# Products of zeros on TensorE ahead of four blocks of a GLA/NSA decoder step

## The chip, the cores and the metric

The kernel runs on one core of a Trainium2 chip. The metric is the device time of one execution in microseconds; of several runs the median counts. All matrix products run on TensorE (PE in the rows), whose granted clock the profile records: 1.00 is 2.4 GHz and 0.50 is 1.2 GHz.

## The reference

One inference step of a two-layer decoder trunk with 512 prompt tokens and 8 decode tokens, width 1024. The first layer mixes with gated linear attention (GLA), the second with native sparse attention (NSA); behind each stands a squared-ReLU MLP of width 4096.

```python
for i in range(DEPTH):                      # DEPTH = 2
    hp = rms_norm(xp, norm_mix[i]); hs = rms_norm(xs, norm_mix[i])
    ...                                     # i = 0: gla_mixer, i = 1: nsa_prompt / nsa_sample
    x = x + mixer(rms_norm(x)); x = x + mlp(rms_norm(x))

def gla_mixer(h, s0, w_in, w_gate2, b_gate, g_out, w_out):
    z = h @ w_in                            # q, k, v, r and the 16 gate-rank columns gr
    log_alpha = log_sigmoid(gr @ w_gate2 + b_gate) / GLA_TAU
    o, s = gla_scan(...)
    o = rms_norm(o, g_out)
    return (o * silu(r)) @ w_out, s

def sq_relu_mlp(h, w_up, w_down):
    u = relu(h @ w_up)
    return (u * u) @ w_down
```

The NSA layer projects h to queries, six kinds of keys and values and the gates, attends in three branches, and ends in `o @ w_out`.

## The kernel before

The 520 tokens lie as columns: the residual `xT` is [128, 8, 520], eight chunks c of 128 channels. Each weight matrix and each activation is split into a high part (fp32r) and a rest, and a block of 128 output columns is the sum of high x high, high x rest and rest x high (`split_products`). A block goes through eight steps k (one chunk of channels each); a step is three products in two halves of 260 tokens, so six matmuls.

TensorE writes into four PSUM slots of two banks. A table made ahead of time gives each product its slot and its turn. `claim` makes TensorE wait until the slot's earlier product has been read, `await_product` is the reader's side. Each engine has its own instruction stream, written out in order; semaphores tie them together.

A norm goes like this: ScalarE squares the chunks, VectorE adds the squares, TensorE multiplies the sum by a matrix of 1/1024 (`mean_square`, line 2038), ScalarE takes the root (line 992), VectorE the reciprocal (line 1469) and then the eight normed chunks (line 1485). ScalarE rounds each chunk to its high part (lines 1023 and 1251). The rest parts of chunks 0 to 3 are made by GpSimd (lines 799 and 876), those of chunks 4 to 7 by VectorE once all eight normed chunks are done (lines 1515 and 1711). TensorE's next block takes them step by step: a wait per k on `mixed_rest_ready[k // 4]`.

Four blocks matter here, in order of time:
- `grank`, the gate-rank block of the GLA layer, behind the first norm: 16 output columns, slot 3; the products `gq` follow. Its weights' rest part comes from GpSimd (line 794).
- `gout` 0, the first block of the GLA output projection, slot 0. Ahead of it stand the last decode products and `omd`, the mean square of the decode rows (line 2185). Its operand needs the last head's norm on VectorE (lines 1469, 1616 to 1636). In the order of TensorE's stream it first waits for its weights (`ow_rest_ready`), then claims, then waits for the operand at k = 0 and again at k = 6.
- `z` 0, the first block of the NSA projection, behind the third norm, slot 0. The weights are ready beforehand.
- `nout` 0, the first block of the NSA output projection, slot 2. Ahead of it stand the turned decode rows `d_ot` (line 2515), their copy on VectorE (line 2008), the high part (line 1451) and the rest (line 2015, `no_rest_ready`).

`identb` is a 128x128 bf16 identity (VectorE, line 1500) and `zerosb` 512 bf16 columns of zeros (GpSimd, line 773); both are made at the start of the kernel. The kernel before already uses such a product in three places to clear a bank.

Of the kernel before, what the change touches and what calls it, by code (L numbers as in the profile page):

```python
# [28 lines left out]
DC = D // 128  # L29
# [68 lines left out]
def trunk(nc, ins, outs):  # L98
    ctx = ExitStack()
    with ctx:  # L100
# [34 lines left out]
        identb = carve("identb", 64).bitcast(BF16)  # L135
        zerosb = carve("zerosb", 256).bitcast(BF16)
# [53 lines left out]
        gh_part = [part("gh_high", at["go"][0], DC, T), part("gh_rest", at["hT"][0], DC, T)]  # L190
# [3 lines left out]
        wgr_part = [part("wgr_high", at["cum"][0], DC, RANK), part("wgr_rest", at["wgr"][0], DC, RANK)]  # L194
# [113 lines left out]
        slot = [ctx.enter_context(nc.psum_tensor(f"slot{s}", [128, 2, 512], F32)) for s in range(4)]  # L308
# [8 lines left out]
        free = [sem(f"free{s}") for s in range(4)] + [sem("free_out_bank"), sem("free_cmp_bank")]  # L317
# [16 lines left out]
        mixed_rest_ready = [sem("mixed_first_rest_ready"), sem("mixed_second_rest_ready")]  # L334
# [273 lines left out]
        def where(name, i=None, n=0):  # L608

            if i is None:  # L610
                return turn[name]
            slots, base, per = turn[name]
            s = n % len(slots)
            return slots[s], i * per + (base[s] + n // len(slots))

        def claim(eng, name, i=None, n=0):

            s, k = where(name, i, n)
            if not isinstance(k, int) or k > 0:
                eng.wait_ge(free[s], k)  # L620
            return slot[s], full[s]
# [1406 lines left out]
        def _(pe):  # L2028
            mm = nc.tensor.matmul
# [12 lines left out]
            def mean_square(n):  # L2042
                pe.wait_ge(sum_ready, DC * (n + 1))
                ps, fu = claim(pe, ("ms", n))
                dense(ps, lambda k: C("mean_d"), lambda k: sq_sum, 1).then_inc(fu, 1)

            pe.wait_ge(ident_in, 32)
            for c in range(DC):
                if c % (DC // 2) == 0:
                    pe.wait_ge(x_in[c // (DC // 2)], 16)  # L2050
                ps, fu = claim(pe, ("xt", c))
# [3 lines left out]
                    .then_inc(fu, 1)  # L2055
            pe.wait_ge(consts_in, 32)
            mean_square(0)
            def split_products(ps, weights, x, wait=None):

                (high, rest), (x_high, x_rest) = weights, x  # L2060
                for k in range(DC):
                    if wait is not None:
                        wait(k)
                    for w, m in ((high, x_high), (high, x_rest), (rest, x_high)):
                        for a in range(2):
                            last = mm(ps[0:w.shape[2], a, 0:HT], w[:, k, :], m[:, k, HT * a:HT * a + HT],  # L2066
                                      start=k == 0 and w is high and m is x_high, stop=k == DC - 1 and w is rest)
                return last

            pe.wait_ge(wgr_rest_ready, 1)  # L2070
            ps, fu = claim(pe, "grank")
            split_products(ps, wgr_part, gh_part, wait=lambda k: pe.wait_ge(mixed_rest_ready[k // 4], k % 4 + 1)).then_inc(fu, 1)

            def gla_products(name, first_block, count):

# [11 lines left out]
            for h in range(GH):  # L2087
                ps, fu = claim(pe, ("gate", h))
# [3 lines left out]
            for n in range(20):  # L2092
# [4 lines left out]
                ps, fu = claim(pe, ("gv", n))  # L2097
                for k in range(DC):
                    high, rest = gw_high2[:, q % 2, k, :], gw_rest2[:, q // 2, k, 256 * (q % 2):256 * (q % 2) + 256]
                    for hp, w in ((0, high), (0, rest), (1, high)):  # L2100
                        last = mm(ps[0:rows, 0, 0:256], gh_part[hp][:, k, 128 * t:128 * t + rows], w,  # L2101
                                  start=k == 0 and w is high and hp == 0, stop=k == DC - 1 and hp == 1)
# [20 lines left out]
            for what, h in GLA_STEPS:  # L2123
                if what == "kt":

                    pe.wait_ge(gdec_ready, h + 1)
                    ps, fu = claim(pe, ("kt", h))
# [3 lines left out]
                elif what == "at":  # L2131

                    pe.wait_ge(kp_ready, h + 1)
                    ps, fu = claim(pe, ("at", h))
                    mm(ps[:, 0, :], identb, zerosb, start=True, stop=False, skip_group_check=True)
                    for c in range(TT):
                        for s in range(NSUB):
# [4 lines left out]
                                      skip_group_check=True)  # L2142
                    last.then_inc(fu, 1)
                elif what == "u":

                    pe.wait_ge(kt_ready, h + 1)
                    ps, fu = claim(pe, ("u", h))
# [4 lines left out]
                elif what == "o":  # L2152
# [3 lines left out]
                    ps, fu = claim(pe, ("o", h))  # L2156
                    for v in range(2):
                        for c in range(TT):
                            o = ps[:, v, 128 * c:128 * c + 128]
                            last = mm(o, gv[:, c, DV * h + 128 * v:DV * h + 128 * v + 128], at2[:, h % 2, c, :],  # L2160
                                      start=True, stop=c == 0)
# [4 lines left out]
                elif what == "vb":  # L2166
# [3 lines left out]
                    ps, fu = claim(pe, ("vb", h))  # L2170
# [3 lines left out]
                elif what == "om":  # L2174
                    pe.wait_ge(osq_ready, h + 1)
                    ps, fu = claim(pe, ("om", h))
# [5 lines left out]
            ps, fu = claim(pe, "omd")  # L2182
# [4 lines left out]
            for n in range(DC):  # L2187
                t, columns = TILE_GLA_OUT + n // 4, slice(128 * (n % 4), 128 * (n % 4) + 128)

                def wait(k):  # L2190
                    if n == 0 and k == 0:
                        pe.wait_ge(go_rest_ready["heads"], 3)
                        pe.wait_ge(go_rest_ready["decode"], 1)
                    elif n == 0 and k == 2 * GH - 2:
                        pe.wait_ge(go_rest_ready["last_head"], 1)

                pe.wait_ge(ow_rest_ready, n + 1)
                ps, fu = claim(pe, ("gout", n))
                split_products(ps, (go_high_w[n % 4], gw_rest2[:, t % 2, :, columns]), go_part, wait).then_inc(fu, 1)
                if n % 4 == 3:  # L2200
                    pe.wait_ge(fu, where(("gout", n))[1] + 1)
                    pe.sem_inc(tile_used[t % 2], 1)
# [23 lines left out]
            for what, n in steps():  # L2226
                kind, j = chunks[n]
                if what == "z":
                    pe.wait_ge(pw_rest_ready, n + 1)
                    ps, fu = claim(pe, ("z", n))  # L2230
                    split_products(ps, pw_part[n % 2], u_part,
                                   wait=(lambda k: pe.wait_ge(mixed_rest_ready[k // 4], DC // 2 + k % 4 + 1)) if n == 0 else None).then_inc(fu, 1)
                elif what == "nm":
                    pe.wait_ge(z_ready, n + 1)
                    ps, fu = claim(pe, ("nm", n))
                    dense(ps, lambda k: C("mean_h"), lambda k: sq4[:, n % 4, :], 1).then_inc(fu, 1)
                elif what == "sw":
                    pe.wait_ge(normed, turned[n] + 1)
                    ps, fu = claim(pe, ("sw", n))
                    dense(ps, lambda k: C("swap"), lambda k: z4[:, n % 4, :], 1).then_inc(fu, 1)  # L2240
                elif what == "gt":
                    pe.wait_ge(pw_rest_ready, len(chunks) + 1)
                    ps, fu = claim(pe, ("gt", 0))
                    split_products(ps, [w[:, :, 0:48] for w in pw_part[0]], u_part).then_inc(fu, 1)
                elif what == "gates":
                    pe.wait_ge(z_ready, len(chunks) + 1)
                    ps, fu = claim(pe, ("gates", 0))
                    for t in range(5):
                        rows = 128 if t < TT else NS
                        last = nc.tensor.transpose(ps[0:rows, 0, 48 * t:48 * t + 48], z4[0:48, 0, 128 * t:128 * t + rows],  # L2250
                                                   ident[0:48, 0:48])
                    last.then_inc(fu, 1)
                else:
                    if is_roped[n]:
                        pe.wait_ge(roped, turned[n] + 1)
                    pe.wait_ge(z_ready, n + 1)
                    src = nk[:, {4: 0, 5: 1, 8: 2, 9: 3}[j], :] if j in (4, 5, 8, 9) else z4[:, n % 4, :]
                    ps, fu = claim(pe, ("tok", n))
                    for t in range(TT):
                        nc.tensor.transpose(ps[:, 0, 128 * t:128 * t + 128], src[:, 128 * t:128 * t + 128], ident)  # L2260
                    nc.tensor.transpose(ps[0:NS, 1, 0:128], src[:, NP:T], ident).then_inc(fu, 1)

            for what, r, sp in compression_steps():
# [4 lines left out]
                if what == "pb":  # L2268

                    pe.wait_ge(pe_sum_ready, r + 1)  # L2270
                    ps, fu = claim(pe, ("pb", r))
                    for c in range(2):
                        last = mm(ps[:, 0, c:c + 1], pe_sum[:, 128 * c:128 * c + 128], C("tri")[:, 127:128],
                                  start=True, stop=True)
                    last.then_inc(fu, 1)
                elif what == "x":
                    pe.wait_ge(st_copied, 8 * r + sp + 1)
                    ps, fu = claim(pe, ("xt2", r, sp))
# [4 lines left out]
                elif what == "m":  # L2283
# [5 lines left out]
                    for half in range(2):  # L2289
                        for wp, xp in ((0, 0), (0, 1), (1, 0)) if g == 4 else ():  # L2290
                            last = mm(psh[:, 0, 0:256], xt_part[xp][:, sp % 2, half:half + 128],
                                      w1_part[wp][:, 8 * half + sp, :], start=sp == 0 and half == 0 and wp == xp,
                                      stop=sp == 7 and half == 1 and wp == 1)
                        for c in range(2) if g < 4 else ():
                            for wp, xp in ((0, 0), (0, 1), (1, 0)):
# [3 lines left out]
                                          stop=sp == 7 and half == 1 and wp == 1)  # L2299
# [4 lines left out]
                elif what == "ht":  # L2304
                    s, k = where(("hid", r))
# [4 lines left out]
                elif what == "c":  # L2310
# [3 lines left out]
                    ps, fu = claim(pe, ("c", r))  # L2314
# [13 lines left out]
                elif what == "cn":  # L2328
                    pe.wait_ge(kcz_ready, r + 1)
                    ps, fu = claim(pe, ("cn", r))  # L2330
# [8 lines left out]
            for what, n in attention_steps():  # L2339
                if what == "cs":  # L2340
                    p, t = n // 4, n % 4
                    ps, fu = claim(pe, ("cs", n))
                    sc = ps[:, 0, 0:2 * GQ * CW]
                    mm(sc, identb, hidden_b[:, t:t + 1, :].to_broadcast([128, 2 * GQ, CW]), start=True, stop=False,
                       skip_group_check=True)
                    for g in range(GQ):
                        last = mm(sc.rearrange("p (e g n) -> p e g n", e=2, g=GQ)[:, :, g, :],
                                  nq[:, 4 * p + g, 128 * t:128 * t + 128], kcz[:, p, :], start=False, stop=g == GQ - 1,
                                  skip_group_check=True)
                    last.then_inc(fu, 1)  # L2350
                elif what == "ct":
                    pe.wait_ge(pc_ready, n + 1)
                    ps, fu = claim(pe, ("ct", n))
# [4 lines left out]
                elif what == "s":  # L2358
# [6 lines left out]
                    ps, fu = claim(pe, ("s", n))  # L2365
                    scores = both_kinds(ps, t)
                    kinds = [slice(0, 2)] if t < 2 else [slice(0, 1), slice(1, 2)]
                    for part in (ks_high, ks_rest):
                        for a in kinds:
                            mm(scores[:, a, :], qs[:, n // 8 % 2, e, g, :], part[e][:, p, a, 0:w], start=part is ks_high,  # L2370
                               stop=False, skip_group_check=True)
                    for a in kinds:
                        last = mm(scores[:, a, 128 * t:128 * t + 128], identb,
                                  future_b.unsqueeze(1).to_broadcast([128, a.stop - a.start, 128]), start=False, stop=True,
                                  skip_group_check=True)
                    last.then_inc(fu, 1)
                elif what == "t":
                    pe.wait_ge(p_ready, n + 1)
                    ps, fu = claim(pe, ("t", n))
# [7 lines left out]
                elif what == "pv":  # L2387
                    p, t, g, _ = unit(2 * n)
# [125 lines left out]
            for m in range(8):  # L2514
                last = mm(ps[:, 0, 32 * m:32 * m + 32], o_rows[:, 128 * m:128 * m + 128], fold, start=True, stop=True)
            last.then_inc(fu, 1)
            pe.wait_ge(no_rest_ready, DC + 1)
            for n in range(DC):
                t, columns = TILE_NSA_OUT + n // 4, slice(128 * (n % 4), 128 * (n % 4) + 128)
# [114 lines left out]
```

## Time and profile before

| | us |
|---|---|
| median of three runs | 1972.5 |
| lowest, highest | 1971.04, 1978.53 |
| the profiled execution | 1968.85 |
| its span | 1967.1 |
| TensorE busy | 1790.7 |
| VectorE, ScalarE, GpSimd busy | 895.2, 678.4, 446.3 |
| mean granted clock of TensorE | 0.946 |

All times inside the profile count from the start of the span. A busy TensorE is not one at its peak: a matmul's recorded length contains its way through the array and overlaps with the next one, so the distance from start to start tells the pace.

### The profile page before, as it was taken

To read this page: it belongs to the slowest core of one execution; us is meant where nothing else is said; L and a number is where in the kernel's file an instruction comes from. 1 tells how busy PE (TensorE), PEld (TensorE's weight loads), DVE (VectorE), ACT (ScalarE), POOL (GpSimd) and SP (SyncE) were. 2 spreads that over 40 slices of the span, in tenths; PEclk is the share of its full clock that TensorE was granted. 3 is DMA by queue.
4 is the path that set the end of the run, shared out by engine and by line. 5 is a ranking of instruction groups with operands and counts; after the bars stand their busy time and mean duration, and the time that the engine had idled before them with its cause. 6 is when DMAs were issued, how large, how long until landed. Compare 5 with 4: busy or idle time off the path is not lost.

```text
span 1967.1 us, 32578 instructions
## 1 busy us (share of the span) xinstructions
PE 1790.7 (91%) x13592; PEld 1626.9 (83%) x13592; DVE 895.2 (46%) x1347; ACT 678.4 (34%) x1131; POOL 446.3 (23%) x381
## 2 busy tenths in 40 slices
PE   4999997999999997999799998898877999999996
PEld 2989876999999997989677786676644999999996
DVE  6051254744444345446622523877422644434343
ACT  3353233332313232323233422777641332313230
POOL 3244224100000002334212221787702100000000
PEclk9999777999999998999899999899987999999998
DMA  4122122223222221241221210001463322222211
GB/s 161 44 86 86 46 85 95 96 87 116 89 87 87 87 87 50 75 143 63 80 92 54 86 54 1 1 1 44 171 258 129 129 86 87 86 87 86 87 44 44
DMA packets 22254, 166.26 MB, mean 85 GB/s; under 512 B 2112, under 2 KB 9840, under 8 KB 12568
## 3 DMA queue, kind: packets, MB, share of 16 engines
q1 hardware_dynamic: 17896, 122.60, 16.7%
q0 software_dynamic: 4208, 41.45, 5.7%
q8 instruction: 120, 1.97, 0.4%
q14 instruction: 30, 0.25, 0.0%
HBM read 154.00 MB, written 10.04 MB: 83 GB/s over the span
## 4 chain that ended last, share of the span: by engine, by line
PE 79%; DVE 9%; ACT 5%; issue 3%; DMA 2%; POOL 1%; ACTq 0%; DVEq 0%; SPq 0%; PEldq 0%; POOLq 0%
PE slot L2066 53%; PE slot L2297 9%; PE slot L2038 2%; PE slot L2280 2%; ACT phase L1374 2%; PE slot L2140 1%; POOL phase L923 1%; DVE normed_x L1485 1%; PE slot L2172 1%; PE slot L2101 1%; DVE phase L1469 1%; PE slot L2426 1%; PE slot L2397 1%; PE slot L2118 1%; PE slot L2382 1%
## 5 line engine op out<-in xcount | busy, mean ns | idle before, releaser
L1198 ACT ACTIVATE w_high<-weights 128x1024 fp32r<-128x1024 f32 x128 | 135.3, 1060 | 258.1 <-PE slot L2066 250.0
L2066 PE MATMUL slot<-h_high,w_high 128*128 128x260 f32 x1024 | 210.5, 287 | 12.1 <-issue 12.1
L2066 PE MATMUL slot<-h_high,w_rest 128*128 128x260 f32 x1024 | 209.0, 286 | 2.8 <-issue 2.8
L2066 PE MATMUL slot<-h_rest,w_high 128*128 128x260 f32 x1024 | 208.8, 286 | 0.0
L2066 PE MATMUL slot<-u_high,w_high 128*128 128x260 f32 x1024 | 206.3, 283 | 0.0
L2066 PE MATMUL slot<-u_rest,w_high 128*128 128x260 f32 x1024 | 206.0, 283 | 0.0
L2066 PE MATMUL slot<-u_high,w_rest 128*128 128x260 f32 x1024 | 205.9, 283 | 0.0
L1665 DVE TENSOR_TENSOR w_rest<-weights,w_high 128x1024 fp32r<-128x1024 f32 x128 | 156.1, 1222 | 31.1 <-ACT w_high L1198 31.1
L2066 PEld LDWEIGHTS slot<-h_high,w_high 128*128 128x128 f32 x1024 | 160.7, 192 | 10.7 <-issue 10.3
L2066 PEld LDWEIGHTS slot<-h_rest,w_high 128*128 128x128 f32 x1024 | 160.5, 192 | 5.7 <-issue 5.7
L2066 PEld LDWEIGHTS slot<-h_high,w_rest 128*128 128x128 f32 x1024 | 160.3, 191 | 0.0
L865 POOL TENSOR_TENSOR pw_rest<-weights,pw_high 128x1024 fp32r<-128x1024 f32 x20 | 48.0, 2401 | 485.7 <-ACT pw_high L1181 469.1
L2066 PEld LDWEIGHTS slot<-u_rest,w_high 128*128 128x128 f32 x1024 | 157.8, 188 | 0.0
L2066 PEld LDWEIGHTS slot<-u_high,w_rest 128*128 128x128 f32 x1024 | 157.8, 188 | 0.0
L2066 PEld LDWEIGHTS slot<-u_high,w_high 128*128 128x128 f32 x1024 | 157.6, 188 | 0.0
L923 POOL TENSOR_SCALAR phase<-phase 128x128 f32<-128x128 f32 (+3 forms) x128 | 140.5, 1115 | 45.0 <-DVE phase L1478 44.9
L1685 DVE TENSOR_TENSOR phase<-phase 128x520 f32<-128x520 f32 x64 | 44.9, 701 | 202.3 <-ACT phase L1229 202.3
L1689 DVE TENSOR_TENSOR phase<-slot,base 128x520 f32<-128x520 f32 x64 | 44.8, 700 | 186.3 <-PE slot L2066 186.3
L1229 ACT ACTIVATE phase<-slot 128x520 f32<-128x520 f32 x64 | 38.8, 607 | 259.4 <-PE slot L2066 259.4
L2297 PE MATMUL slot<-xt_high,w_high 128*128 128x512 f32 x256 | 107.9, 421 | 4.7 <-DVE xt_rest L1799 4.7
L1799 DVE TENSOR_TENSOR xt_rest<-slot,xt_high 128x512 fp32r<-128x512 f32 (+1 forms) x80 | 48.9, 611 | 134.0 <-ACT xt_high L1305 133.2
L2297 PE MATMUL slot<-xt_rest,w_high 128*128 128x512 f32 x256 | 102.0, 398 | 0.0
(370 smaller groups left out, 3804.6 us busy)
## 6 DMA issues: line engine op xcount, KB each, us to landing
weights<-in_wt SPq DMA_DIRECT2D x47, 2048.0 KB, 8.5
weights<-in_state SPq DMA_DIRECT2D x2, 2048.0 KB, 8.6
out<-weights POOLq DMA_DIRECT2D x2, 2048.0 KB, 8.8
weights<-in_w SPq DMA_DIRECT2D x2, 2048.0 KB, 8.8
phase<-in_v_win SPq DMA_DIRECT2D x4, 1024.0 KB
out<-phase SPq DMA_DIRECT2D x6, 512.0 KB, 9.3
phase<-in_x_prompt SPq DMA_DIRECT2D x2, 1024.0 KB, 6.3
weights<-in_k_win SPq DMA_DIRECT2D x2, 1024.0 KB, 7.1
```

The source lines that it names most:

```text
L865: nc.gpsimd.tensor_tensor(pw_part[n % 2][1][:, :, :], ring[:, t % 2, :, 128 * (n % 4):128 * (n % 4) + 128], pw_part[n % 2][0][:, :, :].bit ...
L923: last = nc.gpsimd.tensor_scalar(rows, rows, small[:, 8 * (n % 4) + 6 + a:8 * (n % 4) + 7 + a], None, ALU.mult)
L1198: nc.scalar.activation(w_part[k % 4][0][:, :, :], ring[:, s, :, 128 * (k % 4):128 * (k % 4) + 128], ACT.Copy).then_inc(w_high_ready, 1)
L1374: ins_ = nc.scalar.activation(pst[:, n % PST, a, 0:w], scores[:, a, :], ACT.Exp, scale=HD ** -0.5, bias=small[:, 8 * (n % 4) + a:8 * (n % ...
L1665: nc.vector.tensor_tensor(w_part[k % 4][1][:, :, :], ring[:, s, :, 128 * (k % 4):128 * (k % 4) + 128], w_part[k % 4][0][:, :, :].bitcast(F ...
L1685: nc.vector.tensor_tensor(u, u, u, ALU.mult).then_inc(usq_ready, 1)
L1689: nc.vector.tensor_tensor(halves(gx), tok(ps), halves(rstd_sq), ALU.mult).then_inc(scale_ready, 1)
L1799: nc.vector.tensor_tensor(xt_part[1][:, sp % 2, 0:w], ps[:, 0, 0:w], xt_part[0][:, sp % 2, 0:w].bitcast(F32), ALU.subtract).then_inc(xt_re ...
L2038: last = mm(ps[0:weights(k).shape[1], a, 0:HT], weights(k), moving(k)[:, HT * a:HT * a + HT], start=k == 0, stop=k == chunks - 1)
L2066: last = mm(ps[0:w.shape[2], a, 0:HT], w[:, k, :], m[:, k, HT * a:HT * a + HT], start=k == 0 and w is high and m is x_high, stop=k == DC - ...
L2280: last = nc.tensor.transpose(ps[:, 0, nr * h:nr * h + nr], st2[0:nr, sp % 2, 128 * h:128 * h + 128], ident[0:nr, 0:nr])
L2297: last = mm(psh[:, c, 0:KV * nr], w1_part[wp][:, 8 * half + sp, 128 * c:128 * c + 128], xt_part[xp][:, sp % 2, half:half + KV * nr], start ...
```

## The change

The change defines `zero_products(ps, n)`, n matmuls of `identb` with `zerosb` into bank 0 of a slot that the following block claims and then overwrites. They are placed: 16 ahead of `grank`, and 10 in its middle at k = 4 into slot 2, after a wait that the mean square there has been read; 20 ahead of `gout` 0, behind its claim and ahead of its wait for the operand; 22 ahead of `z` 0, behind its claim; 5 ahead of `nout` 0, whose claim is also made earlier, ahead of the wait on `no_rest_ready`.

```diff
+            def zero_products(ps, n):
+
+                for _ in range(n):
+                    mm(ps[:, 0, :], identb, zerosb, start=True, stop=True, skip_group_check=True)
+
...
             pe.wait_ge(wgr_rest_ready, 1)
             ps, fu = claim(pe, "grank")
-            split_products(ps, wgr_part, gh_part, wait=lambda k: pe.wait_ge(mixed_rest_ready[k // 4], k % 4 + 1)).then_inc(fu, 1)
+            zero_products(ps, 16)
+
+            def wait_for_rest(k):
+                if k == DC // 2:
+                    pe.wait_ge(free[2], where(("ms", 0))[1] + 1)
+                    zero_products(slot[2], 10)
+                pe.wait_ge(mixed_rest_ready[k // 4], k % 4 + 1)
+
+            split_products(ps, wgr_part, gh_part, wait=wait_for_rest).then_inc(fu, 1)
...
                     if n == 0 and k == 0:
+                        zero_products(ps, 20)
                         pe.wait_ge(go_rest_ready["heads"], 3)
                         pe.wait_ge(go_rest_ready["decode"], 1)
...
                     ps, fu = claim(pe, ("z", n))
+                    if n == 0:
+                        zero_products(ps, 22)
                     split_products(ps, pw_part[n % 2], u_part,
...
             last.then_inc(fu, 1)
+            ps, fu = claim(pe, ("nout", 0))
+            zero_products(ps, 5)
             pe.wait_ge(no_rest_ready, DC + 1)
```

## Rows read from the trace of the kernel before

**Rows 1.** The page: busy time of the engines, and the clock in 40 slices.
```profile
PE 1790.7 (91%) x13592; PEld 1626.9 (83%) x13592; DVE 895.2 (46%) x1347; ACT 678.4 (34%) x1131; POOL 446.3 (23%) x381
...
PEclk9999777999999998999899999899987999999998
```
**Rows 2.** The chain of waits at four places: start, length, engine and line.
```profile
45.85 27.23 PE slot L2066 x210
...
337.48 7.61 PE slot L2066 x51
...
787.27 8.92 PE slot L2066 x72
...
1511.01 19.11 PE slot L2066 x144
```
**Rows 3.** Stretches: length, busy time by engine, granted clock, DMA share, GB/s.
```profile
37.90:39.80 1.90, 0.00 (x0) 0.00 (x0) 1.90 (x1) 0.26 (x1) 1.90 (x2) 1.00 0.00 0
39.90:43.00 3.10, 0.00 (x0) 0.00 (x0) 3.10 (x3) 0.64 (x1) 3.10 (x2) 0.50 0.00 0
45.80:50.10 4.30, 4.25 (x20) 3.04 (x21) 1.21 (x2) 0.13 (x1) 0.00 (x0) 0.50 0.01 4
...
337.50:340.20 2.70, 2.70 (x12) 2.70 (x13) 1.22 (x1) 1.47 (x2) 1.15 (x1) 0.50 0.98 419
340.30:345.00 4.70, 4.70 (x41) 4.70 (x41) 0.23 (x1) 0.00 (x0) 1.22 (x1) 1.00 0.03 10
767.70:770.30 2.60, 0.00 (x0) 0.00 (x0) 1.70 (x3) 0.64 (x1) 0.00 (x0) 1.00 0.05 8
770.40:772.80 2.40, 2.10 (x4) 1.18 (x4) 0.23 (x1) 0.00 (x0) 2.09 (x1) 0.50 0.40 121
...
780.40:784.00 3.60, 3.56 (x13) 2.97 (x14) 3.60 (x3) 1.28 (x2) 3.60 (x3) 0.50 0.00 0
784.00:787.20 3.20, 1.81 (x12) 1.39 (x12) 3.20 (x5) 1.84 (x3) 1.38 (x1) 1.00 0.00 0
...
1511.00:1514.40 3.40, 3.39 (x15) 3.39 (x16) 0.00 (x0) 0.00 (x0) 0.00 (x0) 0.50 0.02 5
...
217.00:323.00 106.00, 102.80 (x534) 78.72 (x533) 50.19 (x83) 40.48 (x62) 31.41 (x27) 0.73 0.16 55
```
**Rows 4.** Timeline of TensorE around the gate-rank block: start, length, line, tiles, idle before.
```profile
22.19 2.07 PE L2038 MATMUL slot<-base 128*128 128x260 f32 x4 [5.27 <-DVE base L1497]
31.93 0.59 PE L2066 MATMUL slot<-gh_high,wgr_high 128*16 128x260 f32 x2 [7.66 <-POOL gh_rest L799]
...
37.46 0.40 PE L2066 MATMUL slot<-gh_high,wgr_rest 128*16 128x260 f32 x2
43.06 0.62 PE L2066 MATMUL slot<-gh_high,wgr_high 128*16 128x260 f32 x2 [5.20 <-DVE gh_rest L1515]
...
47.13 0.64 PE L2066 MATMUL slot<-gh_high,wgr_high 128*16 128x260 f32 x2
...
48.43 0.64 PE L2066 MATMUL slot<-gh_high,wgr_high 128*16 128x260 f32 x2
```
**Rows 5.** Timeline of TensorE: two products of zeros in the decode part.
```profile
1474.51 0.59 PE L2482 MATMUL slot<-base 128*128 128x512 bf16 x2 [1.41 <-ACT phase L1436]
```
**Rows 6.** Timeline of TensorE ahead of the GLA output projection.
```profile
327.78 1.06 PE L2185 MATMUL slot<-phase,base 128*128 128x32 f32 x4 [0.43 <-ACT phase L1157]
```
**Rows 7.** Timeline of TensorE around the first NSA projection block.
```profile
770.69 2.10 PE L2038 MATMUL slot<-base 128*128 128x260 f32 x4 [3.09 <-DVE base L1497]
...
780.38 0.77 PE L2066 MATMUL slot<-u_high,pw_high 128*128 128x260 f32 x2 [7.59 <-POOL u_rest L876]
...
788.09 0.41 PE L2066 MATMUL slot<-u_high,pw_high 128*128 128x260 f32 x2
...
788.80 0.40 PE L2066 MATMUL slot<-u_high,pw_high 128*128 128x260 f32 x2
```
**Rows 8.** Timeline of TensorE ahead of the NSA output projection.
```profile
1505.99 3.59 PE L2515 MATMUL slot<-phase 128*128 128x32 f32 x16 [1.53 <-DVE phase L1999]
```

## The prediction

> **What bounds the kernel now.** I read the page first. TensorE is busy for 91% of the span, no other engine for even half of it, so what TensorE waits for and how fast it is clocked decide the time [rows 1]. Then I took the chain of waits at the four places where the change puts instructions [rows 2]. At each, a stretch on VectorE, ScalarE or GpSimd ends and a long unbroken run of TensorE products begins: at 45.85, 337.48, 787.27 and 1511.01 us. Nothing on TensorE hides what comes ahead of those runs, and everything after one shifts with it. Third, the stretches with their granted clock [rows 3]. The clock has two levels, 1.00 (2.4 GHz) and 0.50 (1.2 GHz). One step of a block (one k: three products in two halves, six matmuls) takes 1.30 us at the low level (47.13 to 48.43 [rows 4]) and 0.71 us at the high one (788.09 to 788.80 [rows 7]). So each microsecond that such a run spends at the low level costs 0.59/1.30 = 0.45 us. That is what the change can win, and only where the run is on the chain.
>
> The reader should see when the clock moved [rows 3]. It fell between 39.8 and 39.9 us, 2.0 us after the last product had ended at 37.86, and between 770.3 and 770.4, some 2.7 us after TensorE had gone idle ahead of 767.7. It rose at 340.2, 2.8 us after dense work had begun at 337.48; at 784.0, 3.6 us after 780.38; it was still low at 50.1, 4.3 us after 45.85, and at 1514.4, 3.4 us after 1511.01. So the lag differs from place to place: 2.8 to 4.3 us for a rise, 2.0 to 2.7 us for a fall. I use these as bounds; where a change of level falls relative to the work is not fixed. One caution: the row 31.93 [rows 4] lies in a stretch that reads 1.00 because the clock's records only begin later; its pairs follow one another as slowly as those at 47.13, so the level was low there too.
>
> **The change part by part.** It adds 73 products of a bf16 identity with 512 zero columns and two waits, and moves one claim up. It removes nothing, and no DMA and no other engine's instruction moves. Price of a zero product at the high level: two of them take 0.59 us together with 0.376 us for each one alone, so they start 0.21 us apart [rows 5]. At the low level no row shows one; 260 columns take 1.30/6 = 0.217 us [rows 4], so 512 take an estimated 0.43 us. The extra weight loads overlap.
>
> *Place A, 16 products ahead of the gate-rank block, 10 in its middle.* The operands of the first 16 are there: TensorE is held only by its own mean-square product, which ends at 24.26 us [rows 4], and slot 3 was emptied long before. Even all at the low level they take 6.9 us, to 31.1, still ahead of the 31.93 at which the first step's data arrive. With a rise after 2.8 to 4.3 us, 7 to 10 run slow and the rest fast: they end between 29.0 and 29.9. Steps 0 to 3 come as GpSimd delivers them, 1.7 us apart; faster products there gain nothing, because step 4 waits for VectorE until 43.06. The 10 inner ones start near 37.7 and take 2.1 to 4.3 us: done by 42.0 at the latest, hidden too. Their other wait, for slot 2, is for a read long over. The gain can only lie in steps 5 to 7 and the start of the next block: 3 x 0.59 = 1.8 us, and 0.17 us for the next block's first products (0.37 us at the low level up to 50.1), together 1.9 us. But between the inner zeros and step 5 TensorE works only on step 4 (0.7 to 1.3 us) in a stretch of 3.9 to 6.1 us, more idle time than preceded the fall at 39.8. Bounds 0 and 1.9; nearer to the row of that fall, so I take 0.7.
>
> *Place B, 20 products ahead of the GLA output projection.* TensorE ends its last small products at 328.84 [rows 6]; the block needs data at 337.48 [rows 2]. At the low level throughout, 20 take 8.6 us, to 337.4, just in time; with a rise after 2.8 to 4.3 us they end at 334.5 to 335.3 and leave 2.2 to 3.0 us of idling. The block ran 2.8 us at the low level [rows 3], worth 1.2 us; in an execution with the late rise (4.3 us) it would be 1.9. If the clock falls in the remaining gap, the block pays up to 4.3 us of low clock again, 0.7 us more than now. Bounds -0.7 and +1.9; I take 1.2.
>
> *Place C, 22 products ahead of the first NSA projection.* They start at 772.79 [rows 7], right behind the mean-square product that has run since 770.69, so a rise is due after 0.7 to 2.2 us of them; they end at about 777.8 to 778.6, ahead of 780.38. But there is nothing to win: steps 0 to 3 are paced by GpSimd, and in this execution the clock was up from 784.0 [rows 3], before the long run at 787.27 began [rows 2]. There is something to lose. At the low level steps 0 to 3 fill 1.30 of each 1.7 us and the clock rises out of them; at the high level they fill 0.71 and leave a microsecond idle each time. If the clock falls under that pattern, the long run starts low and pays up to 4.3 x 0.45 = 1.9 us. From 784.0 to 787.2 it held at 1.00 with two such steps, so I take the loss at 0.5; bounds 0 and 1.9.
>
> *Place D, five products ahead of the NSA output projection.* TensorE ends the turned rows at 1509.58 [rows 8] and the block begins at 1511.01: 1.43 us. Five products at the low level need 2.15 us, to 1511.73: the block starts 0.7 us late, the one delay that is plain in the rows. In exchange work is dense from 1509.58, so the rise comes at 1512.4 to 1513.9 rather than after 1514.4; the block is low for 0.7 to 2.2 us instead of 3.4, worth 0.5 to 1.2 us. Without an earlier rise it is low for 2.7 and the sum is -0.4. Bounds -0.4 and +0.5; I take +0.2. The claim moved up costs nothing: its slot was emptied before the decode output began.
>
> Sum: 0.7 + 1.2 - 0.5 + 0.2 = 1.6 us gained. Against the profiled execution that is a span of 1967.1 - 1.6 = 1965.5 and, with the 1.75 us around it, 1968.85 - 1.6 = 1967.3. That execution is 3.65 us below the median of the three runs, 1972.5, and I predict for the median: 1970.9.
>
> **Rivals.**
> *All four bursts do their work and the clock stays up into the runs.* 1.9 + 1.9 + 0 + 0.5 = 4.3 us, 1968.2. For it: B's remaining gap, 2.2 to 3.0 us, is about what preceded a fall. Against it: A and C leave more idle time than that.
> *Zero products do not raise the clock.* Then C's 22 take 9.5 us, to 782.3, 1.9 us late, but the four steps catch up and step 4 starts at 787.5, 0.2 us late; D is 0.7 late, A and B are hidden: about +1, 1973.5. The four zero products in the kernel stand alone inside other work, so the rows cannot exclude this.
> *The clock falls again in the idle time behind the zeros (the slower side).* Its place is first C: the level won by the zeros is lost in the idle microsecond of each step, and the run at 787.27 starts low, where now it starts high; that is 1.9 us. The same at B (0.7) and D (0.4) with nothing at A makes 3.0 us: 1975.5. It decides from about 2 us of idling in a short stretch. For it: the falls at 39.8 and 770.3; against it: 784.0 to 787.2.
> The Trainium skill ("TensorE: Matmul & The Clock Gate", section on HAM oscillation) tells of a kernel whose bursts are parted by waits and start slow every time. By that rule C would be this rival; the row 784.00:787.20 disagrees as far as two steps go. The same page (Part 1) says that the number of slow matmuls at the head of a burst varies from run to run of one kernel; the lags of rows 3 agree.
> *The rest of the kernel shifts against the clock.* Between 217 and 323 us the mean clock is 0.73 [rows 3] with TensorE nearly always busy: 57 us are low. An execution that gets another pattern there can be several microseconds off in either direction; to pass 0.5% it would take some 20 us more or fewer at the low level.
>
> **How the numbers follow.** 0.5% of 1972.5 is 9.9 us, about what a measurement of this kernel can tell from no change; no sum of the bounds, -3.0 to +4.3, comes near it. Chances: the forecast (0.5 to 3 us gained) 0.50, all four work 0.12, zeros without effect 0.08, clock falls again 0.20, a shifted pattern elsewhere 0.10. Only the last can leave the half per cent, so: faster 0.06, same 0.90, slower 0.04. The bounds give 1968.2 to 1975.5. The profiled execution lies 3.65 us below its median and the slowest run 6.0 above, which a median of few runs shares in part: 1964.5 to 1977.5.
>
> **What would show each step.** Zero products 0.21 or 0.43 us apart; those of A over by 30, of B by 335.5, of C by 779; D's block 0.7 us late. Granted clock 1.00 at 337.5 to 340.2, and 0.50 in part of 43 to 50. If the run at C starts at 0.50, that term was too small. I am wrong beyond the range if the zeros start later than computed (a claim or weight wait that is not over), since every late microsecond in B or C goes straight into the time, or if a fall in the middle of the kernel moves.

## Result, and the profile after

The changed kernel took 1947.33 us (median of four runs, 1946.73 to 1954.97) against 1974.9 us for the kernel before (four runs, 1971.04 to 1978.53): ratio 0.987, 95% interval 0.9837 to 0.9903. It is 1.3% faster by that ratio, some 26 us, where 1.6 us had been forecast and 1964.5 was the low end of the range. The profiled execution took 1947.02 us with a span of 1945.2, 21.9 us less than that of the kernel before.

The page of the changed kernel, in the lines that answer to [rows 1], and the instruction queue from its third part (packets, MB, share):

```profile
PE 1801.6 (93%) x13656; PEld 1624.9 (84%) x13665; DVE 895.4 (46%) x1347; ACT 678.9 (35%) x1131; POOL 446.2 (23%) x381
...
PEclk8999877999999999999899999799997999999998
...
q8 instruction: 85, 1.39, 0.3%
...
L2071 PE MATMUL slot<-h_high,w_high 128*128 128x260 f32 x1024 | 207.3, 284 | 0.0
L2071 PE MATMUL slot<-h_high,w_rest 128*128 128x260 f32 x1024 | 206.6, 283 | 0.0
```

The same lines of the page of the kernel before, which the prediction had not used:

```profile
q8 instruction: 120, 1.97, 0.4%
...
L2066 PE MATMUL slot<-h_high,w_high 128*128 128x260 f32 x1024 | 210.5, 287 | 12.1 <-issue 12.1
L2066 PE MATMUL slot<-h_high,w_rest 128*128 128x260 f32 x1024 | 209.0, 286 | 2.8 <-issue 2.8
```

The reader should see two things. The first products of the feed-forward blocks had 12.1 and 2.8 us of idle time ahead of them that nothing released ("issue"), and have none now. And 35 packets fewer were fetched on the instruction queue, each 16 KB (1.97 MB in 120).

I took the start of the same VectorE instruction in both traces and followed the difference:

| VectorE instruction | before, us | after, us | saved so far |
|---|---|---|---|
| first feed-forward, line 1685 at the loop's start | 396.80 | 397.14 | -0.34 |
| behind its first jump back | 586.09 | 581.71 | 4.38 |
| behind its second | 681.85 | 674.07 | 7.78 |
| third norm, line 1469 | 773.55 | 764.82 | 8.73 |
| second feed-forward, line 1685 at its start | 1570.83 | 1561.64 | 9.18 |
| behind its first jump back | 1761.60 | 1746.20 | 15.39 |
| behind its second | 1860.39 | 1838.56 | 21.83 |

Each feed-forward runs three of its four panels in a hardware loop (`with pe.Fori(1, PANELS)` in `feed_forward`), so TensorE jumps back twice per layer. (VectorE's loop starts one panel earlier, at its first line 1685.) Those four places give 4.7 + 3.4 + 6.2 + 6.4 = 20.7 of the 21.9 us. None of the four places that the change touches is among them. The chain of waits of the kernel before at the first jump (start, length, what):

```profile
567.95 6.96 PE slot L2066 x58
574.91 1.55 issue
576.47 1.58 PE slot L2066 x11
578.04 1.35 issue
579.40 2.76 PE slot L2066 x12
```

and of the changed kernel around the same place and the next jump:

```profile
559.91 140.10 PE slot L2071 x1166
```

Two pauses interrupt the products, with eleven products between them; then the clock falls as well. The stretches of the kernel before (columns as in [rows 3]):

```profile
486.00:574.80 88.80, 88.80 (x741) 88.70 (x739) 38.23 (x45) 24.97 (x31) 0.00 (x0) 1.00 0.26 96
574.80:579.50 4.70, 1.79 (x13) 1.59 (x13) 2.53 (x3) 1.06 (x1) 0.00 (x0) 0.97 0.22 49
579.50:583.00 3.50, 3.50 (x19) 3.50 (x19) 0.00 (x0) 0.00 (x0) 0.00 (x0) 0.56 0.92 370
```

The 2.9 us of pauses, the slow clock up to 583 and the rest of the restart make the 4.7 us. Last, the DMA queues over the time of the second and third pass of the first loop. Kernel before, 573 to 767 us:

```profile
q1 hardware_dynamic: 1152, 16.78, 23.3%
q8 instruction: 18, 0.29, 0.6%
q14 instruction: 1, 0.01, 0.0%
```

Changed kernel, 568 to 760 us, where the line of q8 is missing, because nothing was fetched on it:

```profile
q1 hardware_dynamic: 1152, 16.78, 23.3%
q14 instruction: 1, 0.01, 0.0%
```

The Trainium skill says what fits here ("Runtime: NRT & Kernel Launch", section "Instruction fetch mechanics"): TensorE's instruction memory holds 128 KiB or 2048 instructions, it is refilled in blocks of 16 KiB, and a taken branch whose target is not held must first fetch it. The packets of 16 KB agree. The page counts a target as held when it lies in the current window of two such blocks; here the trace differs and decides, for in the changed kernel the target lies 1578 instructions back, over six blocks, and nothing was fetched. A body of 1578 instructions is held in one place and not in another.

### The profile page after: what moved, and what is told of

Read it like the earlier page. It is cut to its first block, busy times and chain, and to the rows that moved or that the text cites. A ratio compares the mean times of both kernels' runs of the same rounds, so it can differ in the third digit from the quotient of the medians.

```text
span 1945.2 us, 32715 instructions
## 1 busy us (share of the span) xinstructions
PE 1801.6 (93%) x13656; PEld 1624.9 (84%) x13665; DVE 895.4 (46%) x1347; ACT 678.9 (35%) x1131; POOL 446.2 (23%) x381
## 4 chain that ended last, share of the span: by engine, by line
PE 79%; DVE 10%; ACT 5%; issue 2%; DMA 2%; POOL 1%; ACTq 0%; DVEq 0%; SPq 0%; PEldq 0%; POOLq 0%
PE slot L2071 53%; PE slot L2313 9%; PE slot L2038 2%; PE slot L2296 2%; ACT phase L1374 1%; PE slot L2153 1%; POOL phase L923 1%; PE slot L2185 1%; DVE normed_x L1485 1%; PE slot L2114 1%; DVE phase L1469 1%; PE slot L2413 1%; PE slot L2442 1%; PE slot L2398 1%; DVE base L1469 1%
## 5 line engine op out<-in xcount | busy, mean ns | idle before, releaser
L2313 PE MATMUL slot<-xt_high,w_rest 128*128 128x512 f32 x256 | 101.7, 397 | 0.0
```

The lines of the kernel that those rows point to most:

```text
L2313: last = mm(psh[:, c, 0:KV * nr], w1_part[wp][:, 8 * half + sp, 128 * c:128 * c + 128], xt_part[xp][:, sp % 2, half:half + KV * nr], start ...
```

## Experiments

The "tiny product" of these kernels has one weight column and one zero column, `mm(ps[0:1, 0, 0:1], identb[:, 0:1], zerosb[:, 0:1], ...)`. It has the same two instructions as a product of zeros and next to no work; 46 of them ahead of the first mean square take 1.3 us, in time in which TensorE waits.

**The same instructions without the work.**

```diff
             def zero_products(ps, n):
 
                 for _ in range(n):
-                    mm(ps[:, 0, :], identb, zerosb, start=True, stop=True, skip_group_check=True)
+                    mm(ps[0:1, 0, 0:1], identb[:, 0:1], zerosb[:, 0:1], start=True, stop=True, skip_group_check=True)
```

> The changed kernel with every product of zeros cut to one weight column by one zero column: the same 73 products at the same places, so the same number of TensorE instructions ahead of each feed-forward loop, but next to no work on the array. Theory of place (the gain comes from where the loop bodies lie in TensorE's instruction stream: the pauses at 574 to 579, 671 to 676, 1748 to 1753 and 1847 to 1852 us of the kernel before are instruction fetches and go away): those pauses stay away, the instruction queue moves about 85 packets instead of 120, and the time is 20 us below the kernel before, 1953, within 3 us of the changed kernel. Theory of the clock (the gain comes from the work of the zero products at the four blocks): the time returns to that of the kernel before, 1973, plus or minus 2.

Measured: 1949.74 us against 1972.33, ratio 0.9874 (0.9844 to 0.9904). No pauses, 85 packets. Almost the whole gain is there although the zeros do no work.

**The work of the zeros at the old place.**

```diff
             pe.wait_ge(consts_in, 32)
+            pe.wait_ge(bf_ready, 3)
+            tiny_products(claim(pe, ("ms", 0))[0], 81)
             mean_square(0)
...
+            tiny_products(claim(pe, ("nout", 0))[0], 101)
             for g in range(4):
                 pe.wait_ge(win_in[g % 2], 16 * (g // 2 + 2))
```

> The changed kernel with all its products of zeros, and in addition 81 tiny products (one weight column by one zero column) ahead of the first mean square and 101 ahead of the decode window part, so that both loops start at the old place modulo 256 instructions (74 and 67; before 75 and 68). Their own cost should be under 4 us, as they stand where TensorE waits. Theory of place: the pauses at the loops' jumps back are there again (four pairs of about 1.5 to 3 us) and the time is 1973 to 1978, no faster than before. Theory of the clock: the time stays with the changed kernel, 1948 to 1955.

Measured: 1975.45 us against 1972.33, ratio 1.0013 (0.9993 to 1.0033): nothing is left of the gain. Its page and its waits of TensorE in the two feed-forwards (392 to 766 and 1557 to 1944 us; total, times, longest):

```profile
q8 instruction: 122, 2.00, 0.4%
```
```profile
PE slot L2078 <- issue: 5.1, 3, 1.8
...
PE slot L2078 <- issue: 8.0, 4, 2.5
```

The pauses are back, and all the products of zeros are there. Not all of the lost gain is theirs: the 101 tiny products ahead of the decode window part stand between other products, not in a wait. From the start of the last copy at line 1436 to that of the copy at line 1999 this kernel takes 37.9 us (1472.9 to 1510.8), the kernel before 30.4 (1474.2 to 1504.6), and the ten kernels without tiny products there 30.1 to 33.6. Some 4 to 8 us of its time may thus be the price of the padding; the changed kernel is 27 us faster. These two kernels decide between the theories.

**One loop alone.** The kernel before, with tiny products only:

```diff
             pe.wait_ge(consts_in, 32)
+            pe.wait_ge(bf_ready, 3)
+            tiny_products(claim(pe, ("ms", 0))[0], 46)
             mean_square(0)
...
+            tiny_products(claim(pe, ("nout", 0))[0], 81)
             for g in range(4):
```

> The kernel before, without products of zeros, with 46 tiny products ahead of the first mean square and 81 ahead of the decode window part: the first loop starts at 168 modulo 256 (as in the changed kernel), the second at 67 (as before). Theory of place: the pauses of the first loop go and those of the second stay; about 8 us gained in the first loop and none in the second: 1965 to 1969. Theory of the clock: 1973 to 1976, no gain.

Measured: 1967.48 us, ratio 0.9961 (0.9936 to 0.9987), 4.9 us less. The mechanism is as expected: no waits without a releaser in the first feed-forward, four in the second, 103 packets. The second feed-forward's waits:

```profile
PE slot L2073 <- issue: 8.5, 4, 2.5
```

The gain is smaller than the 8 us of the traces' difference. The interval reaches to 12.6 us and holds it, and the traces show where the rest went: at the first loop's end, 8.1 us are saved (line 1685 from 399.49 to 676.41, before from 396.80 to 681.85), but the stretch from line 1436 to line 1999, with the 81 tiny products in it, takes 36.3 us (1467.7 to 1504.0) instead of 30.4. The expectation had put the padding at nothing.

**The changed kernel beside them.**

> The changed kernel once more, on the chip of the other three, to stand beside them. Both theories: 20 to 26 us below the kernel before, and no pauses at the loops' jumps back.

Measured: 1948.72 us, ratio 0.9886 (0.9852 to 0.992). The zeros' own work is thus worth about 1 us against the tiny products (1949.74), less than the intervals can tell from nothing.

**Other starting places.** The kernel before with 9, 20, 103 or 117 tiny products ahead of the first mean square, one run of each, so that their traces tell more than their times:

```diff
             pe.wait_ge(consts_in, 32)
+            pe.wait_ge(bf_ready, 3)
+            tiny_products(claim(pe, ("ms", 0))[0], 9)
             mean_square(0)
```

> The kernel before with 9 tiny products (one weight column by one zero column) ahead of the first mean square: the loops start at 94 and 87 modulo 256 instructions (before: 75 and 68, with pauses; changed kernel: 167 and 214, without). A loop body is 1578 instructions, 6 times 256 and 42. Theory of place, narrow form (a loop is held if it touches seven pieces of 256 instructions, and paused if it touches eight): the starts that pause form one stretch 42 wide that holds 68 and 75, so it begins at 34 to 68 and ends at 75 to 109; 87 and 94 can fall on either side and bound it. Wide form: pauses in a stretch wider than 42. With pauses the time is near 1972, without near 1951.

> As the one above with 20 tiny products: starts at 116 and 109 modulo 256. Narrow form: no pauses in either loop, about 85 instruction packets, a time near 1951. Wide form: pauses, near 1972.

> As above with 103 tiny products: starts at 26 and 19. Narrow form: no pauses in either loop, near 1951. Wide form: pauses, near 1972.

> As above with 117 tiny products: starts at 54 and 47. Narrow form: together with the starts 94 and 87 this bounds the stretch; if 94 and 87 are free of pauses, then 54 and 47 pause, if 94 and 87 both pause, then 47 does not. Wide form: pauses in both and at 87 and 94 too.

Measured beside 1975.65 us for the kernel before: 1965.88, 1949.09, 1954.97 and 1955.63 us. The wide form as expected, with pauses at all these places, falls. But the sentence on 94/87 and 54/47 missed too, since it put the starts of both loops on one scale. With starts at 94 and 87 only the first loop pauses; with 54 and 47 only the second. The waits without a releaser, starts 94 and 87, first feed-forward (there is none in the second), and the page's queue line:

```profile
PE slot L2073 <- issue: 7.5, 4, 2.2
```
```profile
q8 instruction: 102, 1.67, 0.3%
```

Starts 54 and 47, second feed-forward (there is none in the first):

```profile
PE slot L2073 <- issue: 5.8, 4, 1.9
```
```profile
q8 instruction: 103, 1.69, 0.3%
```

All the starts seen, modulo 256, by my count:

| | pauses | none |
|---|---|---|
| first loop | 74, 75, 94 | 26, 54, 116, 167, 168 |
| second loop | 47, 67, 68 | 19, 87, 109, 214 |

By this count the pausing stretch lies between 54 and 116 for the first loop and between 19 and 87 for the second, and the two seem offset. The offset is an error of the count. A product of two fp32 operands stands in the trace twice (line 2038 in [rows 4]: x4 for a product in two halves), and I had counted it once. The trace of the kernel before has 302 matmuls more than the count ahead of the first loop and 782 more between the loops, so the starts move by 604 and 2168 instructions, 92 and 120 modulo 256:

| | pauses | none |
|---|---|---|
| first loop | 166, 167, 186 | 3, 4, 118, 146, 208 |
| second loop | 167, 187, 188 | 78, 139, 207, 229 |

Now one stretch answers for both loops: it lies between 146 and 207, is at least 23 and at most 60 wide, and no start contradicts it. The 42 of the narrow form (a body that touches eight blocks instead of seven) fits and would be one in six places. That it is just 42 was not measured, nor where the blocks begin, since what is loaded ahead of the kernel's first instruction is not in the count.

A pause does not always cost the same. One pass takes 92.3 us without one (581.71 to 674.07 in the changed kernel) and 95.4 to 98.8 with one; the kernel with starts at 54 and 47 pays only 6.8 us for its two jumps, the one that moved the first loop alone 12.4 for the same two.

**What the zeros themselves do.** Two kernels with the instruction places of the changed kernel, the first with tiny products in place of the 22 ahead of `z` 0, the second with zeros only ahead of `gout` 0:

```diff
                     if n == 0:
-                        zero_products(ps, 22)
+                        tiny_products(ps, 22)
```

> The changed kernel with the 22 products of zeros ahead of the first NSA projection block cut to tiny ones (one weight column by one zero column), the other 51 as they are; instruction positions unchanged. By the profiles so far the zeros at this place cost 0.6 us on average (the stretch from the last normed chunk to the reading of the first block took 3.87, 5.77 and 3.83 us with them, 3.84, 3.85 and 3.84 without). Theory of place: 20 to 26 us below the kernel before, within 2 us of the changed kernel, and that stretch at 3.9 us. If the zeros here raised the clock usefully: 1 to 2 us slower than the changed kernel.

```diff
-            zero_products(ps, 16)
+            tiny_products(ps, 16)
...
-                    zero_products(slot[2], 10)
+                    tiny_products(slot[2], 10)
...
-                        zero_products(ps, 22)
+                        tiny_products(ps, 22)
...
-            zero_products(ps, 5)
+            tiny_products(ps, 5)
```

> The changed kernel with only the 20 products of zeros ahead of the GLA output projection left as they are, the other 53 cut to tiny ones; positions unchanged. Theory of place: 20 to 25 us below the kernel before, no pauses at the loops' jumps back. In the profile the first output block from its operand to its reading takes 6.2 us as with all zeros (7.4 to 8.9 without), the first norm block 9.4 to 9.5 as without. Theory of the clock: most of the 20 us is lost again.

Measured: 1949.84 us, ratio 0.9882 (0.9851 to 0.9913), and 1949.35 us, ratio 0.9886 (0.9859 to 0.9913). Both keep the gain; neither can be told from the changed kernel, and no kernel tried is clearly faster than it. What single zeros do shows in the stretches of the profiles, over all twelve traces. From the end of the last normed chunk (A, C) or of the decode rest part (B, D) to the next block's first product (A) or the first block's reading (B, C, D), us:

| | without working zeros | mean | with | mean | gained |
|---|---|---|---|---|---|
| A `grank` | 9.08 to 9.48, eight | 9.34 | 7.75, 8.95, 9.47, 7.75 | 8.48 | 0.9 |
| B `gout` | 7.44, then 8.86 to 8.94, seven | 8.71 | 6.15 to 6.19, five | 6.17 | 2.5 |
| C `z` | 3.83 to 3.87, nine | 3.85 | 3.87, 5.77, 3.83 | 4.49 | -0.6 |
| D `nout` | 7.49 to 7.67, 8.62, 8.89, eight | 7.88 | 7.17 to 7.72, four | 7.36 | 0.5 |

Together 3.3 us. At D the two highest values, 8.62 and 8.89, belong to the two kernels with tiny products there; against the other six (7.59 on average) the zeros gain 0.2 us, not 0.5. At B the changed kernel's trace has 19 recorded products of zeros and full clock from the block's first product on. Timeline of TensorE, then stretches:

```profile
332.27 6.87 PE L2061 MATMUL slot<-base 128*128 128x512 bf16 x19 [0.22 <-issue]
340.68 0.48 PE L2071 MATMUL slot<-go_high,go_w_high 128*128 128x260 f32 x2 [1.54 <-DVE go_rest L1633]
```
```profile
337.50:341.00 3.50, 1.96 (x10) 0.87 (x9) 2.61 (x7) 1.26 (x3) 0.00 (x0) 0.99 0.90 304
341.00:346.00 5.00, 5.00 (x44) 5.00 (x43) 1.23 (x1) 1.18 (x2) 2.48 (x1) 1.00 0.49 210
```

Without zeros (here with starts at 116 and 109) the same block is slow for 6.2 us, not for the 2.8 of [rows 3]:

```profile
340.40:346.50 6.10, 6.05 (x28) 6.08 (x29) 1.23 (x1) 1.55 (x2) 2.46 (x1) 0.50 0.47 199
346.60:349.00 2.40, 2.40 (x22) 2.40 (x21) 0.00 (x0) 0.00 (x0) 0.00 (x0) 1.00 0.00 0
```

The loss at C, in the changed kernel's second profile. The zeros are over, steps 0 and 1 come 1.7 us apart, and the second has already the slow pace:

```profile
763.78 5.46 PE L2061 MATMUL slot<-base 128*128 128x512 bf16 x21 [0.22 <-issue]
771.06 0.51 PE L2071 MATMUL slot<-u_high,pw_high 128*128 128x260 f32 x2 [1.82 <-POOL u_rest L876]
772.77 0.80 PE L2071 MATMUL slot<-u_high,pw_high 128*128 128x260 f32 x2 [0.73 <-POOL u_rest L876]
...
778.06 0.80 PE L2071 MATMUL slot<-u_high,pw_high 128*128 128x260 f32 x2 [0.17 <-DVE u_rest L1711]
```
```profile
769.00:772.00 3.00, 1.18 (x8) 0.78 (x6) 3.00 (x4) 1.87 (x4) 2.73 (x2) 1.00 0.00 0
772.00:776.00 4.00, 3.22 (x13) 2.73 (x12) 4.00 (x3) 1.51 (x3) 4.00 (x3) 0.52 0.00 0
776.00:780.00 4.00, 3.77 (x16) 3.31 (x16) 4.00 (x8) 1.27 (x2) 0.16 (x1) 0.50 0.00 0
```

## Why the prediction was wrong

**The step that failed** is in the first paragraph of the change part by part: "It removes nothing, and no DMA and no other engine's instruction moves." The instructions of TensorE itself moved, both loops among them, and with them the fetches on the instruction queue. Everything behind rested on that sentence, and "only the last can leave the half per cent" most of all. No rival had this mechanism. The term that was put at nothing, the four jumps back, was worth 20.7 us in the two traces, and the pair of kernels with tiny products and with the old places shows that it makes the result, but for about 1 us.

The trace of before had the clue. Idle time with the releaser "issue", 12.1 us on one row of the page, is time in which TensorE waited for nothing that an engine produces. I took it for small change of a group of 1024 and did not ask at which places it stood. It was eight pauses at four jumps. I read only the four places that the change touches, which is right for its direct cost and blind to what depends on where the code behind it lies.

**The terms of the clock** have their size about right, and the sum is too small. A: 0.7 forecast, 0.9 measured; in two of four traces the clock stayed high to the end of the block, in two it fell. B: 1.2 forecast, 2.5 measured, and beyond the upper bound of 1.9, because the block is usually slow for 6.2 us without zeros; 4.3 us, the longest lag that I had found, was no bound. In all five traces with zeros the clock was high from the block's first product, so the remaining idle time, 1.54 us in the row above against the 2.2 to 3.0 computed, never cost anything. C: -0.5 forecast, -0.6 measured, as one loss of 1.9 us in three traces. The rival of the falling clock is thus true at this place and in some executions only. D: 0.2 forecast; measured 0.2 against the kernels that have nothing there and 0.5 against all; the block started 0.14 us later against its operand than before, not 0.7 late. The zeros' first product starts before the recorded end of the product ahead of it, and I had counted from that end. The size of B also shows how far one execution can mislead: without zeros this block took 7.44 us in the one trace that I had, and 8.86 to 8.94 in the six others.

**The rivals.** That zero products do not raise the clock is refuted: at the low level the changed kernel's zeros at A follow at 0.43 us, then the clock reads 1.00 with only zeros running. Timeline, and stretches:

```profile
24.08 2.34 PE L2061 MATMUL slot<-base 128*128 128x512 bf16 x5
26.64 2.47 PE L2061 MATMUL slot<-base 128*128 128x512 bf16 x10 [0.22 <-issue]
```
```profile
23.90:26.90 3.00, 2.78 (x7) 1.06 (x7) 1.78 (x1) 2.45 (x3) 0.49 (x1) 0.50 0.00 0
26.90:29.10 2.20, 2.20 (x10) 0.78 (x8) 2.16 (x2) 1.19 (x2) 0.00 (x0) 0.99 0.00 0
```

Five products take 2.34 us and ten 2.47, the estimate of 0.43 and the 0.21 of [rows 5]. That a pattern of the clock shifts elsewhere is real and small: from the start of `gq` to that of `gout` the traces of all kernels take 287.8 to 297.8 us, and the trace of before was the shortest of them. That is why 1.7 us gained at A and 1.3 at B did not show ahead of the first loop (-0.34 in the table of the result).

## What to carry to other kernels

Before costing an edit, look whether a hardware loop lies behind it in the same engine's stream; if the loop's body is long (1578 instructions here; no other length was tried), its place can decide whether it is fetched again at every jump, and an edit anywhere ahead moves it. Idle time whose releaser is "issue", and a count of packets on the instruction queue that grows with the loop's passes, show it. Then test the edit's work and its place apart: the same number of instructions without the work, and the work with the old place restored by padding. Put the padding where the engine waits, and read its price from the trace: here 46 tiny products in a wait cost nothing, and 81 between other products went with a stretch 5.9 us longer. Count instructions as the trace has them, not as the code has them.

## What the runs showed of the hardware

- A loop of 1578 TensorE instructions ran its second and third pass with no fetch at all, or (kernel before) with 18 fetches of 16 KB and pauses of 2.9 to 4.5 us at each jump back, depending on where it starts.
- A pause of some 3 us costs more than itself: the clock can fall behind it. At the first jump 2.9 us of pauses cost 4.7 us in all.
- Products of zeros raised the clock: at 26.9 us, with only zeros running since 24.3, it went from 0.50 to 0.99. The same numbers of tiny products, 0.03 us apart and so over within 0.8 us, did not: the kernel with all of them tiny has A at 9.47 and B at 8.94 us. Longer rows of them were not tried for this.
- A product of two fp32 operands is recorded as two matmuls and two weight loads: 302 such products ahead of the first loop, 302 records more than products in the code.
